# Rope columns in f32 column groups from the raw residual, query sums as rows, and the latent keys' rope rows on GpSimd

## The reference

```python
h = modulate(rmsnorm_2(x, g_attn_norm), sh_a, sc_a)      # h * (1 + sc) + sh
proj = jnp.dot(h, w_in)
q_lat, kv_lat, k_rope, ca_qkv = jnp.split(proj, split_pts, axis=-1)   # 256, 128, 32, 3 * 512
q = jnp.dot(rmsnorm_2(q_lat, g_q_latent), w_q_up)        # 8 heads of 96
kv = jnp.dot(rmsnorm_2(kv_lat, g_kv_latent), w_kv_up)    # 8 heads of 64 + 64
k = concatenate([k_nope, broadcast(k_rope)], -1)         # 64 + 32
q, k = rmsnorm_2(q, g_mla_q), rmsnorm_2(k, g_mla_k)      # over 96
q, k: the last 32 of 96 are turned by rope (cos, sin of the positions)
```

## Time and profile before

| | |
|---|---|
| median of 3 runs | 1178.46 us |
| profiled execution, its own time | 1179.01 us |
| span of the profile | 1177.3 us |
| TensorE busy | 1167.2 us, 99% |
| weight loads | 958.3 us, 81% |
| VectorE | 566.3 us, 48% |
| ScalarE | 515.5 us, 44% |
| GpSimd | 455.8 us, 39% |
| granted clock of TensorE | full in all slices |

### The profile page before, as it was taken

How to read it: one execution, slowest core, us unless ns; L and a number is a source line. 1 busy time by engine, 2 the same in 40 slices (tenths; PEclk the granted TensorE clock), 3 DMA queues, 4 the chain that set the end, 5 groups by cost and what they waited for, 6 DMA issues and landing times.

```text
span 1177.3 us, 16124 instructions
## 1 busy us (share of the span) xinstructions
PE 1167.2 (99%) x5962; PEld 958.3 (81%) x5962; DVE 566.3 (48%) x1128; ACT 515.5 (44%) x815; POOL 455.8 (39%) x181
## 2 busy tenths in 40 slices
PE   9999999999999999999999999999999999999998
PEld 7787778988888888888988667789888888888887
DVE  4364245977777774212574567726434334440000
ACT  5534653634443432322646576835543443431110
POOL 6541314444434433444443211034434433434442
PEclk9999999999999999999999999999999999999999
DMA  8322122554554542223332110122232223212222
GB/s 302 115 82 98 36 103 78 215 188 174 209 204 171 196 156 94 92 95 110 141 134 77 55 37 1 37 72 74 106 108 102 76 107 107 79 66 99 99 98 96
DMA packets 27714, 132.06 MB, mean 112 GB/s; under 512 B 3472, under 2 KB 4880, under 8 KB 18832
## 3 DMA queue, kind: packets, MB, share of 16 engines
q1 hardware_dynamic: 25776, 128.90, 30.6%
q10 hardware_dynamic: 1888, 2.49, 0.7%
HBM read 129.28 MB, written 2.10 MB: 112 GB/s over the span
## 4 chain that ended last, share of the span: by engine, by line
PE 97%; ACT 2%; issue 0%; POOL 0%; DMA 0%; DVE 0%; DVEq 0%; ACTq 0%
PE psum L1550 86%; PE psum L1619 2%; PE psum L1631 2%; PE psum L2070 1%; PE psum L1780 1%; ACT prob L712 1%; PE psum L1883 1%; PE psum L2006 1%; ACT probT L695 1%; PE psum L1984 0%; POOL wl L494 0%; DMA gains_and_h<-x_first 0%; PE psum L1848 0%; PE psum L2014 0%; PE psum L1589 0%
## 5 line engine op out<-in xcount | busy, mean ns | idle before, releaser
L478 POOL TENSOR_TENSOR wl<-raw,wh 128x2048 fp32r<-128x2048 f32 (+1 forms) x88 | 364.6, 4143 | 497.5 <-ACT wh L628 285.0
L1550 PE MATMUL psum<-xh,wh 128*128 128x512 f32 (+1 forms) x1008 | 382.9, 380 | 1.2 <-POOL wl L494 1.1
L1550 PE MATMUL psum<-xl,wh 128*128 128x512 f32 (+1 forms) x1008 | 378.7, 376 | 0.0
L1550 PE MATMUL psum<-xh,wl 128*128 128x512 f32 (+1 forms) x1008 | 378.6, 376 | 0.0
L1196 DVE SCALAR_TENSOR_TENSOR scratch<-psum,cols,scratch 128x511 f32<-128x511 f32 (+1 forms) x176 | 131.6, 748 | 196.4 <-ACT scratch L773 188.4
L1550 PEld LDWEIGHTS psum<-xh,wh 128*128 128x128 f32 x1008 | 189.5, 188 | 40.1 <-issue 3.1
L1550 PEld LDWEIGHTS psum<-xh,wl 128*128 128x128 f32 x1008 | 189.6, 188 | 34.9
L1550 PEld LDWEIGHTS psum<-xl,wh 128*128 128x128 f32 x1008 | 189.7, 188 | 33.9 <-issue 0.2
L628 ACT ACTIVATE wh<-raw 128x2048 fp32r<-128x2048 f32 (+1 forms) x50 | 88.4, 1768 | 243.8 <-PE psum L1550 243.8
L1550 PE MATMUL psum<-acth,wh 128*128 128x512 f32 (+1 forms) x374 | 141.0, 377 | 0.0
L1550 PE MATMUL psum<-actl,wh 128*128 128x512 f32 (+1 forms) x374 | 140.8, 377 | 0.0
(11 more groups left out here) (269 smaller groups left out, 1384.2 us busy)
## 6 DMA issues: line engine op xcount, KB each, us to landing
raw<-stream SPq DMA_DIRECT2D x69, 1024.0 KB, 4.8
ada_raw<-ada SPq DMA_DIRECT2D x48, 512.0 KB, 5.1
raw<-down SPq DMA_DIRECT2D x32, 704.0 KB, 4.0
outT<-gains_and_h SPq DMA_DIRECT2D x8, 256.0 KB, 5.0
gains_and_h<-xT SPq DMA_DIRECT2D x7, 256.0 KB, 6.4
raw<-stream SPq DMA_DIRECT2D x7, 256.0 KB, 6.8
rel<-rel_tiles ACTq DMA_DIRECT2D x1, 1344.0 KB, 8.7
wsT<-w_spatial_T SPq DMA_DIRECT2D x1, 512.0 KB, 6.1
```

The source lines that it names most:

```text
L478: pool.tensor_tensor(wl[slot][:, 0:w], raw[slot][:, 0:w], wh[slot][:, 0:w].bitcast(F32), ALU.subtract).then_inc(lo_done, 1)
L1550: ins = pe.matmul(out, lhs[a], rhs[b], start=first and n == 0, stop=last and n == 2)
```

## The change

In part A the 32 rope columns leave the weight stream. They come by a DMA of their own (w_rope, 8 x 32 columns and a 128x128 matrix of zeros and ones that repeats and exchanges rows), GpSimd multiplies them by the norm's gain modA, and eight f32 products in four column groups of 32 multiply them by the raw residual h, late in normed_pair. ScalarE copies the result, VectorE multiplies it by the norm's root, ScalarE adds the shift (eight one-column products of the weights with the shift, made earlier), and one f32 product with the zero and one matrix sums the four groups and lays out the 128 rows. Chunk "kvq" holds the latent keys and the first query latent tile; chunk "ql" is half as wide and holds the second. The third latent square's low part moves behind the rope products on VectorE.

In part B the squares of four heads are summed in four column groups by one 512-column product each, ScalarE copies the rows, and four f32 transposes turn them; roots are read from every 32nd column. The key heads' rope rows are multiplied by GpSimd, in between its weight quarters.

```diff
-STREAM2 = [("kvr", 1), ("ql", 1), ...
+STREAM2 = [("kvq", 1), ("ql", 1), ...
-    if n == BASE2["mkv"]:
+    if n in (BASE2["ql"], BASE2["mkv"]):
         return CHUNK // 2
@@ gpsimd
             lows(N1, base - 1, DOWN_CHUNK)
+            pool.wait_ge(pos_landed, 32)
+            pool.wait_ge(mod_done, 7)
+            pool.tensor_tensor(rope_weights..., rope_raw..., modA[:, 0, :]...broadcast, ALU.mult).then_inc(mod_done, 1)
...
+            def rope_keys(p):
+                pool.wait_ge(mla.rstd, p + 1)
+                r = scratch[p % 2]
+                for e in range(2):
+                    a, b = HD * e, HD * e + HD
+                    pool.tensor_tensor(mk[64:P, 2 * p + e, :], k_rope[a:b, :], r[a:b, :], ALU.mult).then_inc(mla.k_rope, 1)
+                    pool.wait_ge(mla.k_rope, 2 * p + e + 1)
+            pool.wait_ge(rope.dve, 7)
+            pool.wait_ge(lo_done, n)
+            rope_keys(0)
             for y, x in enumerate((0, 2, 1, 3)):
                 if y < 2:
                     pool.wait_ge(hi_half, y + 1)
-                else:
+                elif y == 2:
+                    ins.then_inc(lo_first, 1)
+                    pool.wait_ge(lo_first, KD + 10)
+                    for p in range(1, PAIRS):
+                        rope_keys(p)
                     pool.wait_ge(hi_done, n + 1)
@@ scalar
             act.dma_start(pos_i, positions.partition_broadcast(P)).then_inc(pos_landed, 16)
+            act.dma_start(scratch[0][:, 0:ROPE_COLS + P], w_rope[:, :]).then_inc(pos_landed, 16)
...
             norm_rsqrt(norm_attn2, 0, eps2_c)
+            act.wait_ge(p2.mm, P2["shift"])
+            act.activation(rope_shift[:, :], SHIFTS, ACT.Copy).then_inc(rope.act, 1)
...
             norm_high(norm_attn2, ...)
+            act.wait_ge(p2.mm, P2["rope_parts"])
+            act.activation(scratch[2][:, :], rope_parts[:, :], ACT.Copy).then_inc(rope.act, 1)
+            act.wait_ge(rope.dve, 2)
+            act.wait_ge(rope.act, 1)
+            act.activation(scratch[2][:, :], scratch[2][:, :], ACT.Identity, bias=rope_shift[:, :]).then_inc(rope.act, 1)
             act.wait_ge(res_down1.h, KD + 1)
             load_rel(0, 0, 2)
             load_rel(1, 2, HEADS)
...
-            split_next(base, p2.mm, P2["rope"])
+            split_next(base, p2.mm, P2["ql"][0])
...
@@ root_keys:   if p >= 2:
                     act.wait_ge(mla.k, p - 1)
+                    act.wait_ge(mla.k_rope, 2 * p - 2)
...
+            def copy_sums(g):
+                act.wait_ge(mla.ssq, 2 * g + 1)
+                act.activation(sum_rows[:, :], QUERY_SUMS[:, :], ACT.Copy).then_inc(mla.rows, 1)
@@ order: copy_sums(0) before root_keys(1); copy_sums(1) beside step 3; root_heads(1) beside step 6 (was 5)
@@ vector
+            dve.wait_ge(rope.act, 2)
+            for j in range(2):
+                dve.tensor_tensor(scratch[2][:, half(j)], scratch[2][:, half(j)], rstd(j), ALU.mult).then_inc(rope.dve, 1)
...
-            for b, sq in enumerate((sq2[0], sq2[1], scratch[3])):
-                lat_square_low(b, sq)
+            lat_square_low(0, sq2[0])
+            lat_square_low(1, sq2[1])
             ... (k_rope from rope_tile, as before)
+            lat_square_low(2, scratch[3])
@@ key_heads
-                for e in range(2):
-                    a, b = HD * e, HD * e + HD
-                    ins = dve.tensor_tensor(mk[64:P, 2 * p + e, :], k_rope[a:b, :], r[a:b, :], ALU.mult)
@@ tensor
+            def quarter_products(out, columns, moving, ready, value):
+                pe.wait_ge(ready, value)
+                for x in range(KD // QUARTERS):
+                    for quarter in range(QUARTERS):
+                        k, c = QUARTERS * x + quarter, GATE_COLS * quarter
+                        ins = pe.matmul(out[c:c + GATE_COLS, :], columns[:, GATE_COLS * k:GATE_COLS * k + GATE_COLS], moving(k),
+                                        start=x == 0, stop=x == KD // QUARTERS - 1)
+                return ins
@@ residual_down, last tile
+                        if (j, e, kk) == (1, 0, 0):
+                            quarter_products(SHIFTS, rope_raw, lambda k: mod[:, 0, k:k + 1], mod_done, 8).then_inc(p2.mm, 1)
@@ normed_pair, before k-step 6 of the second half
+            def rope_products():
+                pe.wait_ge(norm_attn2.lo, 2 * KD - 2)
+                quarter_products(rope_parts, rope_weights, lambda k: h[:, k, :], mod_done, 8).then_inc(p2.mm, 1)
...
-            for e in range(2):
-                features_tile(bank[2 + e], (base + 1) % 2, e).then_inc(p2.mm, 1)
+            pe.wait_ge(rope.dve, 2)
+            for k in range(KD):
+                if k == KD // 2:
+                    pe.wait_ge(rope.act, 3)
+                    pe.matmul(rope_tile[:, :], rope_turned, scratch[2][:, :], start=True, stop=True).then_inc(p2.mm, 1)
+                ins = split_product(ql_tiles[1][:, :], weights((base + 1) % 2, P * k, P * k + P), inputs(k), k == 0, k == KD - 1)
...
+            def query_sums(g):
+                pe.wait_ge(mla.sqq, EARLY * (g + 1))
+                for x in range(EARLY):
+                    c = SUM_ROWS * x
+                    ins = pe.matmul(QUERY_SUMS[c:c + SUM_ROWS, :], ones[0:96, 0:SUM_ROWS], square_q[x][0:96, :], start=True, stop=True)
+            def turn_sums(g):
+                pe.wait_ge(mla.rows, g + 1)
+                for i in range(TB):
+                    ins = pe.transpose(QUERY_SUMS[:, P * i:P * i + P], sum_rows[:, P * i:P * i + P], ident2[:, :])
@@ order: query_sums(0) after key_sums(1), turn_sums(0) after key_sums(2); query_sums(1) beside step 3, turn_sums(1) beside step 5
@@ latent_ready
+                if step % TB == 0:
+                    pe.wait_ge(mla.k_rope, 2 * (step // TB) + 2)
```

More of the change, by code:

```diff
@@ L288, in build @@
         rope = Stage()
-        rope.dve, rope.sq = sems("rope", "dve", "sq")
+        rope.dve, rope.act = sems("rope", "dve", "act")
         head = Stage()
@@ L293, in build @@
         mla = Stage()
-        mla.mm, mla.sqq, mla.sqk, mla.ssq, mla.ssk, mla.root, mla.rstd, mla.rq, mla.q, mla.k, mla.v = sems(
-            "mla", "mm", "sqq", "sqk", "ssq", "ssk", "root", "rstd", "rq", "q", "k", "v")
+        mla.mm, mla.sqq, mla.sqk, mla.ssq, mla.rows, mla.ssk, mla.root, mla.rstd, mla.rq, mla.q, mla.k, mla.k_rope, mla.v = sems(
+            "mla", "mm", "sqq", "sqk", "ssq", "rows", "ssk", "root", "rstd", "rq", "q", "k", "k_rope", "v")
         lat = Stage()
@@ L302, in build @@
               "q": [17, 19, 21, 23], "k": [18, 20, 22, 24]}
-        P2 = {"kv": 1, "rope": 2, "ql": [3, 4], "q": [5, 7, 9, 11], "k": [6, 8, 10, 12], "v_first": 13, "v": [14, 15, 16, 17]}
+        P2 = {"shift": 1, "rope_parts": 2, "kv": 3, "ql": [4, 6], "rope": 5, "q": [7, 9, 11, 13], "k": [8, 10, 12, 14],
+              "v_first": 15, "v": [16, 17, 18, 19]}
         MLA = {name: n + 1 for n, name in enumerate(
@@ L1050, in heads_and_chunks @@
                     square_head(6 + step)
-                if step == TB + 1:
-                    root_heads(EARLY, HEADS)
+                if step == TB - 1:
+                    copy_sums(1)
+                if step == TB + 2:
+                    root_heads(1)
                 if step == TB:
@@ L1566, in features_tile, with normed_pair @@
                 return ins
-            def normed_pair(banks, slot, mm, norm, aside, at=3, quarter0=None):
+            def normed_pair(banks, slot, mm, norm, aside, at=3, quarter0=None, late=None):
                 for j in range(2):
@@ L1574, in normed_pair @@
                             aside()
+                        if j == 1 and k == KD - 2 and late is not None:
+                            late()
                         if quarter0 is not None and j == 0 and k in (0, 2, 4):
@@ L1820, in _ @@
                 features_tile(bank[6 + e], n % 2, e).then_inc(p1.mm, 1)
-            pe.wait_ge(setup1, 10)
             pe.wait_ge(p1.act, 1)
-            for x in range(KD // QUARTERS):
-                for quarter in range(QUARTERS):
-                    k, c = QUARTERS * x + quarter, GATE_COLS * quarter
-                    ins = pe.matmul(bank[4][c:c + GATE_COLS, :], gate_weights[:, GATE_COLS * k:GATE_COLS * k + GATE_COLS], h[:, k, :],
-                                    start=x == 0, stop=x == KD // QUARTERS - 1)
-            ins.then_inc(p1.mm, 1)
+            quarter_products(bank[4], gate_weights, lambda k: h[:, k, :], setup1, 10).then_inc(p1.mm, 1)
             def gate_sum():
@@ L1914, in last_sums @@
             def last_sums():
+                pe.wait_ge(rope.act, 1)
                 norm_sum(norm_attn2, 1, weighted_acc, KD + 2)
@@ L1928, in pair_sums @@
                         pe.wait_ge(lat.lo, 3)
+                        pe.wait_ge(rope.dve, 5)
                     else:
@@ L1944, in _ @@
                         pe.wait_ge(lat.lo, 3)
-                        pe.wait_ge(rope.dve, 3)
                     elif p == 3:
@@ L2045, in _ @@
             key_sums(2)
[L2046 removed]
+            turn_sums(0)
```

(13 more changed lines are left out.)

90 lines of the change are left out of this document (50 added, 40 removed).

## The result

The changed kernel takes 1182.11 us (median of 8 runs, 1181.27 to 1182.62), the kernel before 1178.72 us (8 runs, 1178.18 to 1178.82). The ratio is 1.003, with a 95% interval of 1.0021 to 1.0039. The forecast was 1177.7, with 1180.6 as the upper end of its range.

The account below looks back on a forecast made before the run. TensorE, holding 97% of the chain, was taken as the bound. Terms +1.2 (late pair), +1.0 (shift), -2.9 (up to step 0) and -0.1 (latent steps) gave -0.8: median 1177.7 us, range 1173.6 to 1180.6.

Parts of the forecast that it names:

- (7): First chunk-attention pair: ScalarE's queue delays the weight split, TensorE stands still 4.3 us, pair starts 1.2 us later.
- (4): Eight one-column products for the shift, ahead of the last down tile half: +1.0 us, between 0.45 and 1.8.
- (5): Second latent tile's half-wide chunk: ScalarE's quarters shrink to 0.35 us, low parts come at 0.79 instead of 0.91: -0.5 us.
- (2): Eight f32 rope products in column groups, priced from the gate columns: +1.95 us.
- (13): Latent projections up to step 0: ScalarE's queue nearly sets the stretch, step 0 comes 2.9 us earlier.
- (12): Query sums: two groups of four f32 transposes are added, 0.9 us each.
- (15): Latent keys' rope rows moved to GpSimd, 1.3 us a row; VectorE lost 1.4 per pair but was waiting for ScalarE's roots.
- (14): Latent steps 0 to 5: -0.1 us in sum; moving the heads' roots from step 5 to 6 is free.
- R3: First latent attention steps: late rope rows on GpSimd hold VectorE's scalings, +0.5 us in all, 1179.0; chance 0.07.
- R1: First chunk-attention weights in time after all, as DMA issues overlap the wait on VectorE: -5.1 us, 1173.4; chance 0.25.
- R2: Latent squares' second low held beside GpSimd's next chunk, TensorE's sum waits 1.6 more: +0.8 us, 1179.3; chance 0.11.
- R4: Column groups don't run side by side: +5.0 us for rope products, +2.5 per query group, 1188; chance 0.02.

Follow-up runs that it names:

- e2: Changed kernel plus 16 products of 512 columns, result unread, in TensorE's stop ahead of the first chunk-attention pair: 1179.76 us.
- e1: Changed kernel with ScalarE's order alone changed: final norm's root ahead of the rope copy, four bias-tile DMA issues behind the next chunk's split: 1175.93 us.
- e6: Changed kernel with only the four DMA issues moved behind the next chunk's split: 1177.11 us.
- e8: Changed kernel with the rope rows of the latent keys multiplied by VectorE again instead of GpSimd: 1183.5 us.
- e5: Kernel of e1 with ScalarE splitting the two late weight quarters in latent attention steps 2 and 4 instead of 4 and 5: 1175.44 us.
- e9: Kernel of e5 with the third low part of the latent squares moved ahead of the rope products and rope square on VectorE: 1174.67 us.
- part A's trace: Kernel before with part A alone (rope columns in f32 column groups from the raw residual): 1183.64 us.

## Why the prediction was wrong

**The step that failed is (7).** It found the right chain, the right place and the right stop ("stands still for 4.3 us", measured 4.83), and then priced the stop as the distance between two starts, +1.2. It never asked what TensorE's clock does in a stop. The granted clock fell to 1.2 GHz, and the twelve products behind it cost 2.57 us more. This is a term that the sum put at nothing without a reason, and the largest part of the miss: with the sizes below, +2.6 for the clock, +1.4 for the start, +0.9 at step 8 and +0.3 behind it, less 0.7 in (4) and 0.4 in part B, which went the other way by luck, make up the 4.2 between -0.8 and +3.4. e2 gives the clock's part back with the late start nearly kept (0.46 earlier); e1 and e6 give it back by a shorter stop. None of the rows that I had chosen holds such a stop, so none could show the drop.

**The size of the same step was also off**, 2.63 instead of 1.2. Of the 1.4 missing, 0.6 lies in front: term (5) expected 0.5 from the narrower chunk, but the low parts still came 0.91 apart, although ScalarE's quarters took 0.41. So the length of the quarters did not set that distance, as (5) had it; what does is not shown. VectorE's timeline, after (to the earlier trace rows):

```profile
576.58 0.48 DVE L1163 SCALAR_TENSOR_TENSOR xl<-psum,mod,xh 128x256 fp32r<-128x256 f32 x1
...
577.49 0.48 DVE L1163 SCALAR_TENSOR_TENSOR xl<-psum,mod,xh 128x256 fp32r<-128x256 f32 x1
```

The rope products started at 582.32 and not at 581.3 plus the shift. The other 0.8 is the chain that I copied as 10.59 us from the earlier trace rows: from the shifted copy to the end of the low parts it took 11.43, and its last issue 1.83 instead of 0.72.

**Term (4)** was 1.0 and measured 0.34, below my lower end of 0.45. The products in column groups are much cheaper than the full-width passes of the earlier trace rows. The weight-load rows suggest why: the eight passes of the earlier trace rows load 128 weight columns each, and those loads run from 708.29 to 709.31; the sixteen loads of 32 columns here run from 561.48 to 561.70. That the load is what a one-column pass costs is read from these rows and was not tried. The 0.4 us that (4) worked out and set aside was the better price.

**Terms (2), (3) and (6)** held: 1.85 for the rope products, no wait for VectorE of note.

**Part B, (10) to (13)**: 3.36 up to step 0, forecast 2.9, with a bound of 4.2. Term (12) was too high: the turning costs 0.36 and not 0.9. ScalarE does hold step 0, as (13) had it, but by 0.32 us. **(15)** timed GpSimd well (1.32 a row, forecast 1.3), but said that VectorE had the room anyway; e8 shows that the move pays 1.2 to 1.5.

**(14)** had -0.1, measured 0. What it missed is at step 8, +0.94. The mechanism is R3's, GpSimd holding VectorE's scalings, but from the two weight quarters and not from the rope rows. The prediction took the move of the heads' roots from step 5 to 6 as free and did not follow what it does to the quarter's split, which had stood behind them on ScalarE. Without the roots ahead of it the split ends earlier against the scalings, and GpSimd starts beside them and no longer just behind. e5, with the quarters ahead of the scalings, shows that the meeting is what cost the time; that the moved roots brought it about was not tried by itself.

**The rivals.** R1 (1173.4, the chunk in time) did not happen, but e1 shows what it was worth: the split at 586.0, the kernel at 1175.9. R2 did not show in the changed kernel, since the late pair gave VectorE time; in e1 it cost about 0.5, and e9 took it away. R4 did not happen.

About 0.3 us behind step 8 stays open.

## What to carry to other kernels

When a forecast leaves the busiest engine standing for microseconds, price the stop and then the clock behind it; here 2.97 us of late start cost another 2.57. When a new dependence is put into an engine's queue, everything behind it inherits the wait: look for the work that doesn't need it (here a root whose input was there, and DMA issues that could come 7 us later at no loss) and put it ahead, or behind the work on the path. Removed TensorE work pays only when the next thing it needs comes earlier too.

## What the runs showed of the hardware

- TensorE after a stop: in the traces with 3.59 and 4.83 us of idle time the granted clock fell within the stop and was 0.50 up to 602.0 and 602.5; with 0.56, 1.17 and 1.83 us it stayed at 1.00. In part A's trace (4.65 us) it fell 0.6 us after TensorE had started again, and fewer products were slow. One execution with the stop of 1.83 (1178.51 us, mean clock 0.998) seems to have lost it too.
- Sixteen one-column f32 passes in four column groups took 0.24 us up to the next product (561.48 to 561.72); eight full-width ones, with four times the weight columns each, took 0.90.
- A DMA issue on ScalarE cost 0.4 to 1.83 us of its queue here, beside the instruction ahead (both start at 585.73), but not beside the one behind: four of them make most of the 2.97 us of "issue" before the root.
- VectorE's instructions with both inputs in SBUF were held beside GpSimd's (1.37 us instead of 0.35 beside quarters of about 1.3 each, 4.55 in e1 for a 32x512 subtraction beside a chunk of 4.60), while those that read PSUM kept 0.69 to 0.71 beside it.
